# Three recurrence tiles beside the paged attention, uneven dense groups, and pages issued from three queues

## The reference: what is computed

```
cols = rmsnorm(x) @ w_in                        # split among three head groups
x += w_out @ concat[ GatedDeltaNet (6 heads), DiffAttention (4), RWKV7 (6) ]
x += MemoryCrossAttention(rmsnorm(x))           # 256 memory tokens, 4 heads of 128
x += ConvGLU(rmsnorm(x))                        # d_ff 2816, width-3 causal conv on the gate
kp = k_pool[page_table]; vp = v_pool[page_table]   # DiffAttention of the new tokens:
p = softmax(s);  p[:, :, 0] - lam * p[:, :, 1]     # 64 pages of 128 positions a sequence
```

## Time and profile before

| | us |
|---|---|
| median of 3 runs (lowest to highest) | 5927.17 (5922.1 to 5932.62) |
| profiled execution, device time | 5921.17 |
| its span, first to last instruction | 5919.5 |
| TensorE busy in the span | 5294.7 (89%), mean granted clock 0.917 |
| VectorE, ScalarE, GpSimd busy | 2368.5, 1498.2, 784.4 |
| HBM read and written | 432.76 MB and 49.09 MB, mean 81 GB/s |

### The profile page before, as it was taken

The page is one execution under the profiler, slowest core; times in us unless marked ns, Lnnn a source line. Parts: engine busy times, 40 slices in busy tenths (PEclk is TensorE's granted clock), DMA queues, the critical chain, the costliest instruction groups (busy, mean ns, idle before and its releaser), DMA issues. The chain is left out here.

```text
span 5919.5 us, 91242 instructions
## 1 busy us (share of the span) xinstructions
PE 5294.7 (89%) x34908; PEld 3261.9 (55%) x34908; DVE 2368.5 (40%) x5479; ACT 1498.2 (25%) x3418; POOL 784.4 (13%) x1063
## 2 busy tenths in 40 slices
PE   8988999995777756889999899998999999989998
PEld 5644445554555542565555655565555655657554
DVE  1156655543445436253433534335333443321322
ACT  2235443432223210121212212122122221211212
POOL 0012221111443310110001101011010110100000
PEclk9989999997987855889999899998999989998998
DMA  3111011104776620312223122232233122241332
GB/s 97 48 31 36 29 33 35 35 32 137 227 223 193 181 70 9 105 43 72 86 72 102 51 73 84 77 84 62 73 87 93 54 76 74 75 130 51 95 94 69
DMA packets 729154, 487.80 MB, mean 82 GB/s; under 512 B 78058, under 2 KB 704106, under 8 KB 728687
## 3 DMA queue, kind: packets, MB, share of 16 engines
q1 hardware_dynamic: 677457, 393.53, 23.3%
q0 software_dynamic: 18432, 50.36, 2.9%
q10 hardware_dynamic: 32832, 38.09, 1.9%
HBM read 432.76 MB, written 49.09 MB: 81 GB/s over the span
## 5 line engine op out<-in xcount | busy, mean ns | idle before, releaser
L3368 PE MATMUL s_f_b<-s_f_h,s_f_W 128*128 128x416 f32 x4480 | 1640.8, 522 | 31.1 <-DMA s_f_h<-o_t 22.1
L3368 PEld LDWEIGHTS s_f_b<-s_f_h,s_f_W 128*128 128x128 f32 x4480 | 845.8, 192 | 708.7 <-issue 691.3
L3426 PE MATMUL s_f_b<-s_f_a,s_f_W 128*128 128x416 f32 x1760 | 634.1, 516 | 0.2
L536 PE MATMUL s_p_acc<-s_hT,s_p_W 128*128 128x416 f32 x1600 | 626.3, 539 | 6.9 <-DMA s_p_W<-in_w_in_dram 6.9
L3426 PEld LDWEIGHTS s_f_b<-s_f_a,s_f_W 128*128 128x128 f32 x1760 | 328.5, 190 | 263.5 <-issue 257.4
L536 PEld LDWEIGHTS s_p_acc<-s_hT,s_p_W 128*128 128x128 f32 x1600 | 300.1, 196 | 286.2 <-issue 269.5
L3624 DVE TENSOR_TENSOR s_f_xT<-s_f_xT,s_f_b 128x416 f32<-128x416 f32 x160 | 93.5, 586 | 587.1 <-PE s_f_b L3426 533.3
L3645 POOL TENSOR_TENSOR s_f_ex<-s_f_ex,s_f_mix 128x416 f32<-128x416 f32 x105 | 111.8, 1065 | 1348.9 <-ACT s_f_mix L3454 1348.3
L918 ACT ACTIVATE s_prob<-s_s_ps,s_ntop 128x512 f32<-128x512 f32 (+3 forms) x320 | 196.4, 619 | 368.2 <-DVE s_ntop L969 368.0
L3497 ACT ACTIVATE s_f_raw<-s_f_b 128x416 f32<-128x416 f32 x110 | 56.9, 517 | 774.9 <-PE s_f_b L3368 774.9
L1165 POOL DMA_DIRECT2D s_V<-in_cache_diff_v_dram x384 | 207.6, 541 | 278.5 <-issue 274.9
(11 more groups left out here) (790 smaller groups left out, 8010.0 us busy)
## 6 DMA issues: line engine op xcount, KB each, us to landing
s_f_W<-in_ffn_w_in_dram SPq DMA_DIRECT2D x220, 512.0 KB, 3.9
s_K<-in_cache_diff_k_dram SPq DMA_DIRECT2D x512, 128.0 KB, 2.9
s_V<-in_cache_diff_v_dram POOLq DMA_DIRECT2D x384, 128.0 KB, 3.2
s_f_W<-in_ffn_w_out_dram SPq DMA_DIRECT2D x80, 448.0 KB, 3.8
cols_t<-s_p_out ACTq DMA_DIRECT2D x100, 208.0 KB, 1.9
s_f_W<-in_w_out_dram SPq DMA_DIRECT2D x40, 512.0 KB, 4.6
s_f_W<-in_ffn_w_out_dram SPq DMA_DIRECT2D x40, 512.0 KB, 4.1
s_V<-in_cache_diff_v_dram ACTq DMA_DIRECT2D x128, 128.0 KB, 3.3
```

Of the source, the lines that this page charges most:

```text
L536: mm = pe.matmul(self.acc[n % 2][:, 0:CH], self.W[:, u, k, :], self.hT[:, k, c * CH:(c + 1) * CH], start=(k == 0), stop=(k == KD - 1))
L3368: mm = pe.matmul(bank(u)[:, 0:G], w[:, k, :], h[:, k, :], start=(k == 0), stop=(k == KD - 1 and kind != "op"))
L3426: mm = pe.matmul(bank(u)[:, 0:G], w[:, k, :], a[:, f % NA, :], start=(k == 0), stop=(k == len(part) - 1))
```

## The change

1. `LEAD` goes from 4 to 3: three tiles of each recurrence run in the paged stage and thirteen in the dense stage.
2. The dense groups become 384, 416, 416, 416 and 448 columns (`GROUPS`); subtiles of a group are a quarter of its prompt columns. Group 0 needs exactly three finished tiles. `spread` now gives each group the tiles that the next one needs: four, three, three, three.
3. Pages: SP issues three K pages of a group and, for even groups, the third V page. ACT issues the fourth K page, the fourth V page and, for odd groups, the third. GpSimd issues the first two V pages. That is 448 pages on SP (before 512), 320 on ACT (128) and 256 on GpSimd (384).

```diff
-LEAD = 4
+LEAD = 3
+GROUPS = (384, 416, 416, 416, 448)
@@ sp_lane of paged_lanes
-            for i in range(4):
+            for i in range(3):
                 sp.dma_start(K[:, g % KG, i, :], kp[page_of(sp, g, i)]...)
+        def v_page(g):
+            if g >= VG:
+                sp.wait_ge(pv, (g - VG) // 4 + 1)
+            sp.dma_start(V_[:, g % VG, 2, :], vp[page_of(sp, g, 2)]...)
...
+            if s in v_slot and v_slot[s] % 2 == 0:
+                v_page(v_slot[s])
@@ pool_lane
-                for i in range(3):
+                for i in range(2):
@@ act_lane
+        def k_page(g):
+            if g >= KG:
+                act.wait_ge(flipped, place[("k", g - KG, 1)] + 1)
+            act.dma_start(K[:, g % KG, 3, :], kp[page_of(act, g, 3)]...)
...
+            for i in (2, 3) if g % 2 else (3,):
+                act.dma_start(V_[:, g % VG, i, :], vp[page_of(act, g, i)]...)
...
                     turn(("k", 16 * b + k, 0))
+                if 1 <= 16 * b + k <= G - KG:
+                    k_page(16 * b + k + KG - 1)
                 if 16 * b + k in v_slot:
-                    v_page(v_slot[16 * b + k])
+                    v_pages(v_slot[16 * b + k])
@@ the dense stage, each instruction of a group c
-                    mm = pe.matmul(bank(u)[:, 0:G], w[:, k, :], h[:, k, :], ...)
+                    mm = pe.matmul(bank(u)[:, 0:G], w[:, k, :], h[:, k, 0:G], ...)   # G = GROUPS[c]
@@ spread
-                        return [t // 3 + 0.92 * ((t % 3) * per + k + 0.5) / (3 * per) for t in ... for k in ...]
+                        for c in range(NCH - 1):
+                            t1 = min(-(-(GROUP_AT[c + 1] + GROUPS[c + 1]) // P), TILES)
+                            n = (t1 - t0) * per
+                            places += [c + 0.92 * (k + 0.5) / n for k in range(n)]
+                            t0 = t1
```

More of the change, by code:

```diff
@@ L39 @@
 NEG = -1.0e30
-LEAD = 4
+LEAD = 3
+GROUPS = (384, 416, 416, 416, 448)
+GROUP_AT = tuple(sum(GROUPS[:c]) for c in range(len(GROUPS)))
+GROUP_P = GROUPS[-1] - NS
 B_QKV, B_Z, B_DIFF, B_RWKV, B_BETA = 0, 9, 12, 18, 29
@@ L1094, in paged_lanes @@
     v_act = [st.sem(f"v_act{j}") for j in range(VG)]
+    v_sp = [st.sem(f"v_sp{j}") for j in range(VG)]
+    k_act = [st.sem(f"k_act{j}") for j in range(KG)]
+    from_sp = lambda g: 16 * sum(o % 2 == 0 for o in range(g % VG, g + 1, VG))
+    from_act = lambda g: 16 * sum(1 + o % 2 for o in range(g % VG, g + 1, VG))
     applied = lambda a: 16 * (a // 4 + 1) + (5, 8, 11, 14)[a % 4]
@@ L1331, in act_lane @@
         act.wait_ge(init, 16)
+        for g in range(KG):
+            k_page(g)
         yield
@@ L3380, in step @@
                 free(pe, u)
-                pe.matmul(bank(u)[:, 0:G], pr.ones[:, :], acc, start=True, stop=True).then_inc(E.sem[kind], 1)
+                pe.matmul(bank(u)[:, 0:G], pr.ones[:, :], acc[:, 0:G], start=True, stop=True).then_inc(E.sem[kind], 1)
             if kind == "sc":
@@ L3416, in step @@
                 for k in range(MH):
-                    mm = pe.matmul(bank(u)[:, 0:G], w[:, k, :], qT[:, k, :], start=(k == 0), stop=(k == MH - 1))
+                    mm = pe.matmul(bank(u)[:, 0:G], w[:, k, :], qT[:, k, 0:G], start=(k == 0), stop=(k == MH - 1))
                 mm.then_inc(E.sem[kind], 1)
@@ L3425, in step @@
                         E.wait(pe, "act", c, f)
-                    mm = pe.matmul(bank(u)[:, 0:G], w[:, k, :], a[:, f % NA, :], start=(k == 0), stop=(k == len(part) - 1))
+                    mm = pe.matmul(bank(u)[:, 0:G], w[:, k, :], a[:, f % NA, 0:G], start=(k == 0), stop=(k == len(part) - 1))
                 mm.then_inc(E.sem[kind], 1)
@@ L3445, in square @@
         def square(c, w, m):
+            G = GROUPS[c]
             n = 8 * w + m
@@ L3449, in square @@
                     E.wait(act, "ns", c, w - 1)
-                act.activation(acc, xT[:, m, :], ACT.Square).then_inc(E.sem["sq"], 1)
+                act.activation(acc[:, 0:G], xT[:, m, 0:G], ACT.Square).then_inc(E.sem["sq"], 1)
                 return
@@ L3472, in step @@
                 E.wait(act, "wq", c, j)
-                act.activation(qT[:, j, :], bank(u)[:, 0:G], ACT.Copy, scale=float(MHD) ** -0.5).then_inc(E.sem["qk"], 1)
+                act.activation(qT[:, j, 0:G], bank(u)[:, 0:G], ACT.Copy, scale=float(MHD) ** -0.5).then_inc(E.sem["qk"], 1)
             if kind == "sc":
@@ L3506, in step @@
                 E.wait(act, "act", c, j - 2)
-                act.activation(val[:, j % 2, :], bank(u)[:, 0:G], ACT.Copy).then_inc(E.sem["vk"], 1)
+                act.activation(val[:, j % 2, 0:G], bank(u)[:, 0:G], ACT.Copy).then_inc(E.sem["vk"], 1)
             if kind == "gap" and j == 7:
@@ L4115, in spread @@
                         per = lane.slots // (TILES - LEAD)
-                        return [t // 3 + 0.92 * ((t % 3) * per + k + 0.5) / (3 * per) for t in range(TILES - LEAD) for k in range(per)]
+                        places, t0 = [], LEAD
+                        for c in range(NCH - 1):
[3 more added lines that the diff above has]
+                            t0 = t1
+                        return places
                     d_at, r_at = spread(D_), spread(R_)
```

109 lines of the change are left out of this document (58 added, 51 removed).

## The result

The changed kernel takes 5966.9 us (median of 10 runs), the kernel before 5925.7 us beside it (10 runs): ratio 1.0067, 95% interval 1.0052 to 1.0082. One of its ten executions took 11564.2 us and is left out of the ratio. The changed kernel is slower by about 40 us; forecast was 33 us faster, and the time lies 22 us above the range.

A forecast was written before the change was run, and what follows sets the result against it. TensorE was taken to bound the dense stage, the paged stage less clearly; paged -97 and dense +64 gave -33 us, from 5921.2 profiled to 5888, stated as a 5893 us median, 8-in-10 range 5830 to 5945.

The forecast's parts named there:

- Ramp -17, tail -18: Paged stage: the 113 us before the first E activation shrink by 17, the 72 us tail by 18.
- Middle (a): Paged stage, first to last E activation: a quarter of TensorE's 175.7 us writing the recurrences' banks goes, -44 us.
- Middle (c): Middle of the paged stage: V pages come later at the fourth apply, 1.4 us at each of 7, +10 us.
- Middle (b): Middle of the paged stage: a quarter of TensorE's 94 us idle outside V waits, at recurrence steps, goes, -24 us.
- (d): Middle of the paged stage: ACT's added page issues delay turns and recurrence copies; with (c) +14 us, bounds -20 to +60.
- Last applies -8: Paged stage's last applies, 51 us: 13 recurrence slots beside the paged ones become 10, -8 us, bounds 0 and -12.
- Thirteenth tile +64: Dense group 0: a fourth tile costs 60 us, between 45 by difference and 68 by load, plus 4 for density.
- Columns zero net: Dense stage: 32 columns moved from group 0 to the last take about 35 us off one and onto the other.
- rival 3: Paged slots with an odd V group: ACT becomes the path and the kernel slower, 5962 us; 0.15 together with rival 4.
- Rival 4: Dense group 0: the tile costs more than 68 us by chain stalls; chance 0.15 together with rival 3.
- Rival 1: Paged middle: SP's issue sets the pace, 588 us falls to perhaps 505, median 5873 us; chance 0.25.
- Rival 2: Paged middle: the 16 DMA engines decide, it becomes 563 us and the total 5923, no change; chance 0.15.

The follow-up runs named there:

- e9: The changed kernel with ACT issuing a slot's V pages ahead of the key copy and K page: 1.0017 to the kernel before.
- e1: The changed kernel with the page issue of before, so tiles and group widths alone: 1.0064 to the kernel before.
- e2: The kernel before with the new page issue alone, four tiles beside the pages and groups of 416: 1.0057.
- e3: The kernel before with only the uneven dense group widths, four tiles beside the pages, pages issued as before: 0.9998.
- e11: The changed kernel with one idle slot between `post` and `back` in the dense tiles of each recurrence: 1.0010 to the kernel before.
- e5: The kernel before with page numbers as constants, so the page table is not read and as many bytes move: 0.9908.
- e6: The changed kernel with page numbers as constants, so the page table is not read: 0.9961 to the kernel before.

## Why the prediction was wrong

Its steps, with the failed one of the middle ahead of the rest of it:

- **Ramp -17, tail -18**: right, -17.6 and -18.1. SP's pages counted one by one gave the first; slots at 3.0 us the second.
- **Middle (a), the tile's work, -44**: right as a size; TensorE's busy time fell by 41.
- **Middle (c), the V waits, +10**: the first failed step; they grew by 37. (c) priced the fourth apply at +10, and it measured +9.4. It took the V wait to be one place, though the earlier trace rows count twelve waits in a middle with seven fourth applies. The others were third applies, which had only a microsecond or two to wait before, and their last group, an odd one with two ACT pages behind a K page, makes each of them wait 3 to 8 us: +26. e9 moves those pages to the front of the slot and gives 535.5 us against the forecast 534, and near its terms: against the middle before, busy time is 40 us less, V waits are 6 more and the other idle time is 19 less, where the forecast had -44, +10 and -20.
- **Middle (b), stalls of the recurrences, -24, and (d), the rest on ACT, +4**: right together, by luck in part. Idle time without the V waits fell by 23 us, where -24 + 4 is -20. In it the waits for key copies rose by 10 (17.2 to 27.0 us over all lines), more than (d) had, and the others fell by 33, more than (b) had.
- **Last applies -8**: failed, +7.5. The fewer recurrence slots are there, but e1, with the old issue, has +12 as well: the end of a tile now falls there. TensorE waits 5.2 us for `s_r_o` and 4.6 for `s_r_ksq` there, and for neither before; a count of slots doesn't see whose long wait lands in a stretch. e2, with the four tiles of before, has +7 there too, which this does not explain.
- **Thirteenth tile +64**: mis-sized, 78.7. The TensorE work, 56.5 by load, was right: busy time grew by 57.2 us over e3's group 0. What was too small is idle time, about 8 us in the forecast (the 60 less the 56.5, and 4 for density) and 20.8 measured. Of it the wait ahead of `back` is 10 more than before; with an idle slot there (e11) idle time falls by 10 and the group by 17. The estimate by difference (45) was the poor bound. "The chain stays hidden" was read from the mean slot of 6.9 us against 3.0, but a wait that stands in TensorE's own order was hidden by nothing behind it.
- **Columns zero net**: right in the medians (e3, 0.9998). e3's profile has -26.3 and +34.6 for the two groups, where the forecast said 35 each; the 9 us between them are within the scatter of one profile.

Of the rivals, rival 3 named the right engine and sign but the wrong place: waits for key copies rose by 10 us, V waits by 37. Rival 4's price above 68 us came true beside it. Rival 1 had a true premise, since e5 gains 0.9% by cheaper issue, but in the changed kernel SP's saving only became SP's waiting. Rival 2 fell by e5 and e6. Two sums of the recorded text don't close: rival 1 takes 75 us off the middle where 588 to 505 is 83, and the prediction's own range ends at 5925 where its upper ends (middle -20, tile 72) add to 9 us above the kernel before, 5936. The measured 5966.9 is outside either. The Trainium skill, "DMA: Bandwidth & Descriptors", section "Issuing engines are not separate DMA queues", holds the sequencer's time to be usually small beside the DMA; here it is not, as e5 alone gains 58 us of 5925 by taking the read of the page number, about 0.5 us, out of each issue. Its other half, that spreading issue buys only that time, agrees with the changed kernel, which got it back in the ramp alone. The chance of 0.14 for slower was too low above all because the sum took each saving as independent of where in-order queues wait.

Open: why the pages cost 34 us alone (e2) but next to nothing beside the removed tile (after against e1). The stages place it in the middle, +42 against +15. Against e1, V waits rise by 38 us and waits for key copies by 11, but the 26 us of K waits and 12 us of others go; alone, there were no K waits to remove, and 15 us of busy time at a lower granted clock came on top. Why the clock fell there is not shown. Open too is the fourth apply of the first sequence, where TensorE waits 9.8 us for V in the changed kernel and 10.9 in e9, and no run took that up.

## What to carry to other kernels

Ask of each DMA that changes engines what stands ahead of it in that engine's order and which consumer's last input it is: the added issues, 1.06 us each and behind a copy, cost a wait at every consumer whose slack was a microsecond, and moving the V pages ahead of the copy and the K page gave 30 us back. Count all the waits of the grouped row, not only the one looked up, since a place with no slack left is the next to wait. A tile moved between stages is worth its marginal price in each, here 57 and 88 us beside the pages against 80 to 90 in the dense group. A slot left free between a long VectorE step and the TensorE work that reads it gave more than any move of a tile (0.33% and 0.57%), but look at idle and busy time apart before saying why: in three-tile groups the wait only moved on, and the busy time fell.

## What the runs showed of the hardware

- Reading a page number from a table in memory costs about half of a page's issue on SP: 1.10 us a page against 0.61 with a constant, while reading a group's four numbers ahead of the DMAs leaves 1.03, as the reads still run one behind the other at about 0.55 us.
- With cheap issue (e6) DMA carried 244 GB/s over the ramp and 226 over the middle, where the kernel before had 150 and 206: the lower rates were no limit of the DMA engines.
- One idle slot beside the 24 or 25 of a dense tile, with no work in it, made the kernel before 0.33% faster (0.20 to 0.46%), with TensorE as idle as before in three-tile groups (34 us against 35). In group 3 its busy time fell from 679.9 to 672.0 us for the same instructions, at a mean granted clock of 0.97 against 0.96.
